# The attention stage of a hybrid GLA/Fourier layer: two products of the first three heads computed as three products of split operands each

## What is computed

```python
scores   = where(mask, einsum('bnihd,bnjhd->bnhij', q_dec, k_inv), 0.0)
o_intra  = einsum('bnhij,bnjhe->bnihe', scores, vc)
d_state  = einsum('bnjhd,bnjhe->bnhde', k_to_end, vc)
s        = decay[..., None] * s + d_state          # carried from chunk to chunk
o_inter  = einsum('bnihd,bnhde->bnihe', q_dec, s_prev)
o        = o_intra + o_inter                       # then forward + backward, per-head RMSNorm
```

## Time and profile before

| what | value |
|---|---|
| median of 3 runs | 1922.58 us |
| time of the profiled execution | 1925.28 us |
| its span, first to last instruction | 1923.5 us |
| TensorE busy | 1869.1 us, 97% |
| VectorE busy | 1208.0 us, 63% |
| ScalarE busy | 941.3 us, 49% |
| GpSimd busy | 647.7 us, 34% |
| mean granted TensorE clock | 0.991 |
| attention stage | about 1170 to 1396 us of the span |

### The profile page before, as it was taken

The page is one execution under the profiler, slowest core; times in us unless marked ns, Lnnn a source line. Parts: engine busy times, 40 slices in busy tenths (PEclk is TensorE's granted clock), DMA queues, the critical chain, the costliest instruction groups (busy, mean ns, idle before and its releaser), DMA issues.

```text
span 1923.5 us, 30195 instructions
## 1 busy us (share of the span) xinstructions
PE 1869.1 (97%) x10393; PEld 1751.3 (91%) x10393; DVE 1208.0 (63%) x2108; ACT 941.3 (49%) x1961; POOL 647.7 (34%) x675
## 2 busy tenths in 40 slices
PE   7899999999999999999999998999999999999997
PEld 2899999999999999999999997888888899997886
DVE  4978777785544435644444464666666667588787
ACT  4565667653445456434455324677742132243343
POOL 0136534034335512444334000000753023443655
PEclk9999999999999999999999999999999999999999
DMA  7578878967888989679788978556456666786443
GB/s 289 211 271 290 283 277 317 380 235 269 283 321 289 319 303 368 222 240 297 249 288 273 336 237 339 218 217 227 176 208 213 200 216 218 240 302 210 163 165 131
DMA packets 174817, 494.78 MB, mean 257 GB/s; under 512 B 15120, under 2 KB 72906, under 8 KB 164300
## 3 DMA queue, kind: packets, MB, share of 16 engines
q1 hardware_dynamic: 160844, 442.53, 66.4%
q10 hardware_dynamic: 13824, 50.34, 6.5%
HBM read 323.98 MB, written 159.39 MB: 251 GB/s over the span
## 4 chain that ended last, share of the span: by engine, by line
PE 62%; DVE 6%; POOL 4%; DMA 3%; issue 3%; ACT 2%; SPq 0%; DVEq 0%; ACTq 0%; POOLq 0%
PE bank L2591 34%; PE bank L2937 8%; PE bank L2891 5%; PE bank L2755 3%; PE bank L2722 3%; PE bank L2820 2%; PE bank L2733 2%; PE bank L2744 1%; DVE me_op L2226 1%; POOL h_lo L1167 1%; POOL yt L1305 1%; POOL yt L1302 1%; DVE me_s L2359 1%; DMA x_st<-in_x 1%; DMA qd<-qk_dec 1%
## 5 line engine op out<-in xcount | busy, mean ns | idle before, releaser
L2591 PE MATMUL bank<-h_hi,w_op 128*128 128x384 f32 x4032 | 1053.6, 337 | 14.4 <-ACT outs L1392 4.7
L2591 PEld LDWEIGHTS bank<-h_hi,w_op 128*128 128x128 f32 x4032 | 733.9, 189 | 20.2 <-issue 20.2
L2591 PE MATMUL bank<-h_lo,w_op 128*128 128x384 f32 x2016 | 676.4, 336 | 0.0
L2591 PEld LDWEIGHTS bank<-h_lo,w_op 128*128 128x128 f32 x2016 | 380.6, 189 | 0.0
L1881 DVE TENSOR_TENSOR w_op<-w_raw,w_op 128x512 fp32r<-128x512 f32 x240 | 189.5, 790 | 90.5 <-ACT w_op L1352 87.8
L1192 POOL TENSOR_TENSOR decs<-decs,qk_s 128x192 f32<-128x192 f32 x192 | 127.1, 698 | 329.7 <-ACT decs L1426 329.4
L1352 ACT ACTIVATE w_op<-w_raw 128x512 fp32r<-128x512 f32 x240 | 149.3, 624 | 160.1 <-PE bank L2591 157.3
L2970 PE MATMUL bank<-ow_op,me_op 128*128 128x512 f32 x756 | 174.3, 391 | 5.1 <-DVE yt L2439 2.5
L2970 PEld LDWEIGHTS bank<-ow_op,me_op 128*128 128x128 f32 x756 | 141.1, 188 | 38.0 <-issue 5.8
L2937 PE MATMUL bank<-op_a,a_op 128*128 128x384 f32 x1008 | 174.9, 334 | 0.0
L2937 PEld LDWEIGHTS bank<-op_a,a_op 128*128 128x128 f32 x1008 | 174.7, 188 | 0.0
(11 more groups left out here) (275 smaller groups left out, 2847.4 us busy)
## 6 DMA issues: line engine op xcount, KB each, us to landing
w_op<-wt_dram SPq DMA_DIRECT2D x192, 512.0 KB, 5.8
wt_dram<-w_op ACTq DMA_DIRECT2D x96, 512.0 KB, 4.8
w_raw<-in_w_in SPq DMA_DIRECT2D x48, 768.0 KB, 6.3
w_raw<-in_w_in SPq DMA_DIRECT2D x24, 1024.0 KB, 6.8
qk_dec<-decs SPq DMA_DIRECT2D x48, 384.0 KB, 6.6
mg_dram<-outs SPq DMA_DIRECT2D x24, 768.0 KB, 7.1
swap<-qk_s SPq DMA_DIRECT2D x48, 192.0 KB, 5.9
v_dram<-outs SPq DMA_DIRECT2D x24, 384.0 KB, 4.9
```

The costliest lines, as they stand in the source:

```text
L2591: ins = pe.matmul(bnk, w_op[slot][:, part, k, :], h[:, j, k, :], start=(first and k == 0 and part == 0 and h is h_hi), stop=(k == HK - 1 a ...
```

## The change

For the run terms of heads 0 to 2 (`RUNS`, 51 of them) and for scores times values in steps 0 to 53 (`NSPLIT` = 54), the one float32 matmul becomes three float32r matmuls. GpSimd splits the values of each step into `v_hi` (a copy) and `v_lo` (a subtraction). The turned keys of a run term are copied by the same ScalarE instruction as before, now to `kin_r` in float32r, and VectorE makes `kin_lo`. ScalarE copies `comb` to `comb_hi` and VectorE makes `comb_lo`. All new tiles are double buffered by step or term; `kin_r` lies where `kin` lies, and four old semaphores are used again. The kept terms, the scores, the products with the states and head 3 stay as they are.

```diff
+            def split_values(s):                              # GpSimd, for s in range(NSPLIT)
+                head, x = STEPS[s]
+                v = v_ld[head % 2][:, chunk_at(head, x), :]
+                if x == 0:
+                    if head == 0:
+                        pool.wait_ge(s_v12, 16)
+                    pool.wait_ge(s_vl[head % 2], (48 if head % 2 else 32) * (head // 2 + 1))
+                if s > 1:
+                    pool.wait_ge(s_o, s - 1)
+                pool.tensor_copy(v_hi[:, s % 2, :], v).then_inc(s_vs, 1)
+                pool.wait_ge(s_vs, V_AT + 2 * s + 1)
+                pool.tensor_tensor(v_lo[:, s % 2, :], v, v_hi[:, s % 2, :].bitcast(F32), ALU.subtract).then_inc(s_vs, 1)
...
+            def high_scores(s):                               # ScalarE
+                if s < NSPLIT:
+                    if s > 1:
+                        act.wait_ge(s_o, s - 1)
+                    act.wait_ge(s_cb, s + 1)
+                    act.activation(comb_hi[:, s % 2, :], comb[:, s % 2, :], ACT.Copy).then_inc(s_cbh, 1)
...
             scale_queries(0)
+            high_scores(0)
...
                 if others:
                     k_out(others[0] + 1)
+                high_scores(s + 1)
...
+            def low_keys(g):                                  # VectorE
+                if g in RUNS:
+                    if g > 1:
+                        dve.wait_ge(s_ds, g - 1)
+                    dve.wait_ge(s_kin, g + 1)
+                    dve.tensor_tensor(kin_lo[:, g % 2, :], bank[turn_bank(g)][:, 0:P], kin_r[:, g % 2, :].bitcast(F32), ALU.subtract
+                                      ).then_inc(s_klo, 1)
+            def low_scores(s):                                # VectorE
+                if s < NSPLIT:
+                    dve.wait_ge(s_cbh, CH_AT + s + 1)
+                    dve.tensor_tensor(comb_lo[:, s % 2, :], comb[:, s % 2, :], comb_hi[:, s % 2, :].bitcast(F32), ALU.subtract
+                                      ).then_inc(s_cbl, 1)
...
                 if s in (0, 1, 2):
                     start_states(s + 1)
+                if s + 1 < len(STEPS):
+                    low_keys(run_term(s + 1))
                 if others:
                     update(others[0])
+                low_scores(s + 1)
...
+                    split = len([r for r in RUNS if r < g])   # TensorE, in turn(g)
+                    if split:
+                        pe.wait_ge(s_klo, K_AT + split)
...
+                if g in RUNS:                                 # TensorE, in state_term(g)
+                    s = NT * head + x
+                    pe.wait_ge(s_klo, K_AT + RUNS.index(g) + 1)
+                    pe.wait_ge(s_vs, V_AT + 2 * s + 2)
+                    out = bank[4 + g % 2][:, 0:DV]
+                    pe.matmul(out, kin_r[:, g % 2, :], v_hi[:, s % 2, :], start=True, stop=False)
+                    pe.matmul(out, kin_r[:, g % 2, :], v_lo[:, s % 2, :], start=False, stop=False)
+                    pe.matmul(out, kin_lo[:, g % 2, :], v_hi[:, s % 2, :], start=False, stop=True).then_inc(s_ds, 1)
+                    return
...
-                pe.wait_ge(s_cb, s + 1)                       # TensorE, in output(s)
-                ins = pe.matmul(out, comb[:, s % 2, :], v_ld[n][:, c, :], start=True, stop=False)
+                if s < NSPLIT:
+                    pe.wait_ge(s_cbl, CL_AT + s + 1)
+                    pe.wait_ge(s_vs, V_AT + 2 * s + 2)
+                    pe.matmul(out, comb_hi[:, s % 2, :], v_hi[:, s % 2, :], start=True, stop=False)
+                    pe.matmul(out, comb_hi[:, s % 2, :], v_lo[:, s % 2, :], start=False, stop=False)
+                    ins = pe.matmul(out, comb_lo[:, s % 2, :], v_hi[:, s % 2, :], start=False, stop=False)
+                else: ...                                     # as before
```

More of the change, by code:

```diff
@@ L198, in build @@
         mid_e = r2("mid_e", [P, 2, HEADS, NT])
+        kin_r = Region(r2.at)("kin_r", [P, 2, P], F32R)
         kin = r2("kin", [P, 2, P])
+        kin_lo = r2("kin_lo", [P, 2, P], F32R)
         pf = r2("pf", [P, 2, DV])
+        comb_lo = Region(r2.at)("comb_lo", [P, 2, P], F32R)
         comb = r2("comb", [P, 2, P])
@@ L212, in build @@
         fin = r2("fin", [P, 2, 2, DV])
+        v_hi = r2("v_hi", [P, 2, DV], F32R)
+        v_lo = r2("v_lo", [P, 2, DV], F32R)
+        comb_hi = r2("comb_hi", [P, 2, P], F32R)
         KEPT_PLACES = [*range(LT - 1, 0, -1), NT - 1, LT]
@@ L247, in build @@
         STEPS = [(head, x) for head in range(HEADS) for x in range(NT)]
+        NSPLIT = NT * (HEADS - 1)
+        RUNS = [g for g, t in enumerate(TERMS) if t[1] == "run" and t[0] < HEADS - 1]
         def place(at, name, shape, dt=F32):
@@ L363, in build @@
         s_tf, s_fac, s_p0 = sem("s_tf"), sem("s_fac"), sem("s_p0")
+        s_vs, s_klo, s_cbh, s_cbl = s_silc, s_gatel, s_gateh, s_rlo
+        V_AT, K_AT, CH_AT, CL_AT = 1, 2, 2, 2 * NP
         s_tr, s_kin, s_ds, s_end, s_pu = sem("s_tr"), sem("s_kin"), sem("s_ds"), sem("s_end"), sem("s_pu")
@@ L1222, in _ @@
                         low_input(p + 1, 1)
+            def split_values(s):
[10 more added lines that the diff above has]
+                pool.tensor_tensor(v_lo[:, s % 2, :], v, v_hi[:, s % 2, :].bitcast(F32), ALU.subtract).then_inc(s_vs, 1)
+            for s in range(NSPLIT):
+                split_values(s)
             def fold(out, a, b, op):
@@ L1554, in k_out @@
                     act.wait_ge(s_tr, g + 1)
-                    act.activation(kin[:, g % 2, :], bank[turn_bank(g)][:, 0:P], ACT.Copy).then_inc(s_kin, 1)
+                    to = kin_r if g in RUNS else kin
+                    act.activation(to[:, g % 2, :], bank[turn_bank(g)][:, 0:P], ACT.Copy).then_inc(s_kin, 1)
+            def high_scores(s):
[4 more added lines that the diff above has]
+                    act.activation(comb_hi[:, s % 2, :], comb[:, s % 2, :], ACT.Copy).then_inc(s_cbh, 1)
             def scale_queries(s):
@@ L2200, in _ @@
             combine_forward(0)
+            low_keys(run_term(0))
+            low_scores(0)
             for s in range(len(STEPS)):
@@ L2742, in output @@
                     pe.wait_ge(s_on, s - 1)
-                pe.wait_ge(s_cb, s + 1)
-                ins = pe.matmul(out, comb[:, s % 2, :], v_ld[n][:, c, :], start=True, stop=False)
+                if s < NSPLIT:
[4 more added lines that the diff above has]
+                    ins = pe.matmul(out, comb_lo[:, s % 2, :], v_hi[:, s % 2, :], start=False, stop=False)
+                else:
+                    pe.wait_ge(s_cb, s + 1)
+                    ins = pe.matmul(out, comb[:, s % 2, :], v_ld[n][:, c, :], start=True, stop=False)
                 reads = [d for d in range(2) if before(d, c) is not None or c < LT]
```

## The result

The kernel before had a median of 1921.83 us (1917.24 to 1924.79, 14 runs), the changed one 1924.20 (1923.30 to 1930.98, 14 runs): a ratio of 1.0018, with a 95% interval of 1.0010 to 1.0027, or 2 to 5 us slower (the two medians are 2.4 us apart). I had forecast 1921.7 and -0.9 us. The profiled execution of the changed kernel had 1930.98 us around a span of 1929.2, the slowest of its runs, so I compare stretches of the stage and not the spans.

A forecast was written before the change was run, and what follows sets the result against it. TensorE was taken to set the pace, with GpSimd delaying VectorE's `low_scores`. Three heads -0.9, chunks 1 to 3 0, head changes +0.8, clock -0.8 gave -0.9: 1922.58 to 1921.7 us, 8-in-10 range 1914.5 to 1931.5.

The forecast's parts named there:

- Chunks 4 to 6: Steps with a second kept term on TensorE: `low_scores` in time, so 3 x -0.14 = -0.4 us a head.
- Ordinary steps: Chunks 7 to 14 of a head: step from 3.05 to 3.01 us, 8 x -0.04 = -0.3 us a head.
- The lock: VectorE's `low_scores` stands still until GpSimd's subtraction is over, ending 0.15 us behind it.
- 2.55 + C: Length in us of an ordinary step when GpSimd's copy of the values takes C, or 2.91 where that is less.
- Chunk 15: Chunk without a run term: gap before `output` grows to 1.79 us, +0.58 - 0.07 = +0.5 us a head.
- Chunks 16 and 17: Gap of 1.75 us before `output` becomes 1.79, the product saves 0.07: -0.1 us together.
- First chunk of heads 1 and 2: `low_scores` behind the scaling of the final state makes `output` 0.3 to 0.45 us late: 2 x +0.4 = +0.8.
- Chunks 1 to 4: Chunks 1 to 3 of heads 1 and 2, 2.51 us each: bounds -0.8 and 0 us, 0 taken.
- The start of head 0: `turn` of step 0 +1.1 us, hidden by chunk 4's load wait; clock behind that wait bounds -1.6 and 0, -0.8 taken.
- Rival 1: GpSimd doesn't matter, copy under 0.36 us or short reads let through: -6.7 us, 1915.9; chance 0.33.
- rival 2: GpSimd's copy costs as much as the subtraction, 0.74 us, step 3.29: +9.6 us, 1932.2; chance 0.22.
- the third case: Sign that the forecast is wrong: TensorE waits for `kin_lo` or `comb_hi` instead of `low_scores`; no size given.

The follow-up runs named there:

- e6: Changed kernel with only scores times values split, every running state term one plain float32 product: 1922.32 us, ratio 0.9997.
- e7: Changed kernel with only the running state terms split, scores times values in plain float32, GpSimd still splitting every chunk's values: 1925.00 us, ratio 1.0010.
- e14: Changed kernel with running terms of chunks 5 to 7 in plain float32, GpSimd's split waiting for `comb_lo`, and `comb_lo(15)` ahead of the update: 1918.36 us, ratio 0.9976.
- e2: Changed kernel with GpSimd splitting the values of steps 0 and 1 only, result not right: 1922.69 us in one execution.
- e3: Changed kernel with GpSimd's split of values for step s also waiting for `comb_lo`, formed by `low_scores(s-1)`: 1922.61 us, ratio 1.0011.
- e13: Changed kernel with the moves of e12 and e3, and `comb_lo(15)` ahead of the kept state's update in chunk 14: 1921.89 us, ratio 0.9993.
- e10: Kernel before the change, with ScalarE's copy of the first kept term behind the normalised output in chunks 4 to 6: 1924.06 us, ratio 1.0002.
- e9: Changed kernel with ScalarE's copy of the first kept term behind the normalised output in chunks 4 to 6: 1925.29 us, ratio 1.0014.
- e12: Changed kernel with the moves of e5 and e9 together: 1926.18 us, ratio 1.0019.
- e5: Changed kernel with TensorE issuing the scores ahead of the turn in steps behind one with two kept terms: 1926.65 us, ratio 1.0017.

## Why the prediction was wrong

**The step that failed** is "Chunks 4 to 6 have a second kept term on TensorE (0.43 + 0.11 us more), so `low_scores` is in time: 3 x -0.14 = -0.4." About `low_scores` it was right: e6 has these steps at 3.6. It did not ask the same of `low_keys`, which I had put down by busy time alone in this kind of step. Measured: +1.17 a head in heads 1 and 2. The chains of waits give the size. The two products save 0.14, and the chain no longer holds `turn_output` and K2's product (0.22 + 0.43): 3.59 - 0.79 = 2.80. It gains `kin_r` 0.29, `kin_lo` 0.30, 0.25 of handing over between 1264.81 and 1265.65, and two turns that had to wait for another engine (one for a copy of ScalarE, one for `kin_lo`) and take 0.26 and 0.30 in place of 0.11: 2.80 + 0.84 + 0.34 = 3.98, where 3.99 was measured. e7 shows the cause by keeping it, e6 and e14 by taking it away. Between forecast and fact lie 1.57 us in each of heads 1 and 2, 3.1 together; in head 0 the steps of the kernel before hold the wait for the load and can't be compared.

**Ordinary steps**: predicted 3.01, measured 2.98, in seven steps a head (I had counted eight, chunk 15's among them). The lock was as predicted (`comb_lo` ending 0.15 us behind GpSimd); only the copy was shorter, 0.407 in place of 0.46, which makes the forecast's 2.55 + C 2.96. e2 and e3 show the lock by its absence: `comb_lo` 0.28 and the step 2.89.

That is also the one place where the Trainium skill (GPSIMD Engine Reference, section 4.1) stood against my term: the copy took 0.407 us, and 0.40 had been the estimate by its rule. The measurement agrees with it; the step by it was 2.95, and it took 2.98.

**Chunk 15**: +0.5 predicted, +0.47 measured. In e3 2.82, in e13 2.42: 0.15 of it is the lock, 0.4 the place behind the update.

**Chunks 16 and 17**: -0.1 predicted, -0.03 measured. I had given both a gap of 1.75 us; chunk 16 has it (3.05 to 2.98), but chunk 17 took only 2.62 before and takes 2.65.

**First chunk of heads 1 and 2**: +0.4 predicted, +0.61 measured. With `comb_lo` alone (e6) the step takes 2.91, the +0.4 of the forecast; with `kin_lo` alone (e7) it takes 2.54 and 2.64. With both, the scaling of the final state is held up by GpSimd's copy (0.51 us for 0.35), `kin_lo` is queued behind it, and the turn waits 0.51 us for `kin_lo`. Where GpSimd stays out of the way (e3) it is 2.77 and 2.84. How the 0.61 divides between them in the changed kernel is not shown.

```profile
1247.01 0.51 DVE L2203 TENSOR_SCALAR fin<-fin,fac 128x256 f32<-128x256 f32 x1
...
1248.06 0.30 PE L2771 MATMUL bank<-consts,kk 128*128 128x128 f32 x1 [0.51 <-DVE kin_lo L2222]
```

**Chunks 1 to 4**: 0 taken, bounds -0.8 us in all; measured -0.50 in each of heads 1 and 2, -1.0 in all and a little outside the bound. `comb_lo` takes 0.29 to 0.51 us there, so it does meet GpSimd, but it comes in time all the same: e3, where the two never meet, has these steps to 0.02 us alike.

**The start of head 0** went otherwise than I had said. The forecast took the later `turn` of step 0 as hidden behind the load, left 1.1 to 1.6 us of that wait, and took -0.8 for the clock. Measured: `turn` waited 1.07 us for `kin_lo`. In steps 1 to 3 `start_states` stands ahead of `low_keys` on VectorE, which I had not looked at, and chunks 1 to 4 of head 0 took 11.04 us where the kernel before has 9.90 (10.75 where the clock stayed up, as in e3). No trace with `kin_lo` in these steps shows TensorE waiting for the load, where the kernel before waited 2.17 us and e10, on the old code, 1.22: the cover was used up. From the first `turn` of the attention to step 6 it is 40.21 us before the change and 38.47 in e10, 37.90 in e6 without `kin_lo`, 40.52 in the changed kernel and 38.62 to 41.01 in the other traces with it. So a loss of about 1 us stands here where the forecast had none, an estimate from single traces.

The clock did fall, only elsewhere: to 0.57 behind the new wait at step 0 instead of 0.52 behind the load. A float32r matmul of 256 columns takes 0.21 us there in the chain of waits and 0.12 to 0.13 two us later. In e10 it did not fall behind the load at all, and the stage from step 0 to step 6 took 18.68 us where the profiled run of before had 21.12 and the changed kernel 19.41: this differs from execution to execution, so the -0.8 stays unproven.

**The sum.** Predicted for a head with its change: -0.3 + 0.5 - 0.1 - 0.4 + 0.4 = +0.1; measured +1.25 = -0.47 (8 to 14) + 0.47 - 0.03 + 1.17 + 0.61 - 0.50. With head 0, from step 6 to step 54 it is +2.62 us (141.75 to 144.37), inside the +2 to +5 of the whole. Rival 1 fell with `comb_lo` at 0.46 us in the ordinary steps, rival 2 with a step of 2.98; the third case, that TensorE waits for `kin_lo`, stood only among the signs that would prove me wrong. So the time landed near the forecast, but in part by luck: the term of chunks 4 to 6 had the wrong sign, and chunks 1 to 4 gave back 1.0 us that I had not counted.

Open: the first step with two kept terms, which stays at 4.0 in e9 and e12 and at 3.72 in e14, was not taken apart. A second PSUM bank or half bank for the turns, which would part them from `kin_lo`, was not tried.

## What to carry to other kernels

When a value is split in two, the second half needs a second read of its source, behind the first. Every buffer that the source lies in stays occupied that much longer: list who waits for that buffer in each kind of step, not in the ordinary one alone, and compare with the cover there. Where two loops share a link, a remedy for one shows little (0.17 us a step in e9, nothing in e5, 0.40 in e14); try taking the link itself away (e14) before reordering around it.

## What the runs showed of the hardware

In the changed kernel 29 of the 54 `comb_lo` (128x128, both operands in SBUF) began while GpSimd's subtraction ran. All ended 0.15 us behind it; they took 0.46 to 0.58 us instead of 0.28. The scaling of the final state in head 1, with one operand in SBUF, ended 0.15 us behind a GpSimd copy and took 0.51 instead of 0.35. `kin_lo`, with one operand in PSUM and one in SBUF, took 0.28 to 0.29 us always, though 10 of the 51 began while GpSimd's subtraction ran and two of them ended before it did. A start order that keeps the two engines apart (e3) makes GpSimd's 1.14 us a step free. The GpSimd copy of 128x256 float32 to float32r took 0.407 us, the subtraction 0.731. A transpose that TensorE had to wait for took 0.26 to 0.30 us in the chain, one that ran on behind others 0.11.
